# A two-block transformer kernel: two weight loads ahead of the key moves, attention values copied bank by bank, mLSTM transposes and convolution low parts moved

## The reference

```python
def hybrid_mixer(hc, hx, w_in, gate_b, mnorm_g, conv_w, w_out, with_ctx):   # first block, layer 0
    q, k, v, o, g, gb, gc, u = jnp.split(h @ w_in, splits, axis=-1)
    ...   # forward and backward mLSTM in chunks, from q, k, v and the gates g
    hn = rms_norm(h.transpose(0, 2, 1, 3), mnorm_g.reshape(ML_HEADS, ML_DV))
    m_out = (hn * sigmoid(o)).reshape(bsz, n, ML_HEADS * ML_DV)
    c_out = gb * short_conv(gc * u, conv_w)
    return jnp.concatenate([m_out, c_out], axis=-1) @ w_out

def attention_mixer(hc, hx, w_in, q_g, k_g, w_out, cos, sin, with_ctx):     # first block, layer 1
    ...   # rms_norm of 16 query and 4 key heads of 64, rope, softmax over 768 keys, @ w_out

def second_block(x, mem, ...):
    ...   # stick-breaking attention, a 31-tap convolution and an SSM side by side, then
    ...   # cross attention to 256 memory tokens, then a gated MLP
```

## Time and profile before

| | us |
|---|---|
| runs shown, median of 3 (lowest to highest) | 2702.88 (2699.74 to 2705.7) |
| the profiled execution, its own time | 2689.14 |
| its span | 2687.4 |
| TensorE busy in it | 2438.8 (91%) |
| VectorE, GpSimd, ScalarE busy | 1492.7, 1128.6, 968.7 |
| mean granted clock of TensorE | 0.953 of full |

### The profile page before, as it was taken

The page is one execution under the profiler, slowest core; times in us unless marked ns, Lnnn a source line. Parts: engine busy times, 40 slices in busy tenths (PEclk is TensorE's granted clock), DMA queues, the critical chain, the costliest instruction groups (busy, mean ns, idle before and its releaser), DMA issues.

```text
span 2687.4 us, 31912 instructions
## 1 busy us (share of the span) xinstructions
PE 2438.8 (91%) x11638; PEld 1970.9 (73%) x11638; DVE 1492.7 (56%) x1997; ACT 968.7 (36%) x1513; POOL 1128.6 (42%) x853
## 2 busy tenths in 40 slices
PE   7999877999999997599989999897888888899999
PEld 6888766888888886466768888676644665688887
DVE  7756756746464634888552122469488444452433
ACT  5212233413131326567452233443444353432322
POOL 1423112535343422277634467355453231344444
PEclk7999988999999998899999999999999899999999
DMA  6333102333333321411222232132200120232323
GB/s 229 128 108 118 40 31 95 118 110 109 109 109 109 109 94 40 108 36 43 75 77 94 95 97 92 60 111 94 94 0 1 55 69 26 73 100 93 101 90 107
DMA packets 68822, 231.69 MB, mean 86 GB/s; under 512 B 8048, under 2 KB 10992, under 8 KB 68592
## 3 DMA queue, kind: packets, MB, share of 16 engines
q1 hardware_dynamic: 68720, 230.35, 26.4%
HBM read 219.57 MB, written 2.10 MB: 82 GB/s over the span
## 4 chain that ended last, share of the span: by engine, by line
PE 48%; issue 25%; POOL 13%; DVE 10%; ACT 3%; SPq 1%; DMA 1%; POOLq 0%; DVEq 0%; ACTq 0%
PE PS L671 33%; POOL HL L530 12%; PE PS L689 5%; DVE RD L2341 2%; PE PS L1115 1%; PE PS L708 1%; DVE ADJ L1964 1%; PE PS L939 1%; DVE SM L2325 1%; PE PS L1208 1%; PE PS L1104 1%; SPq L484 0%; PE PS L1080 0%; PE PS L1123 0%; DMA EARLY<-adastream 0%
## 5 line engine op out<-in xcount | busy, mean ns | idle before, releaser
L530 POOL TENSOR_TENSOR HL<-RAW,HL 128x512 fp32r<-128x512 f32 x614 | 900.8, 1489 | 1374.0 <-ACT HL L1253 1373.6
L671 PE MATMUL PS<-HA,HL 128*128 128x512 f32 (+1 forms) x2592 | 556.4, 367 | 18.1 <-DVE V L2115 5.0
L671 PE MATMUL PS<-HID,HL 128*128 128x512 f32 (+1 forms) x2832 | 561.8, 360 | 0.0
L671 PE MATMUL PS<-HB,HL 128*128 128x512 f32 (+1 forms) x2592 | 540.7, 361 | 0.0
L671 PEld LDWEIGHTS PS<-HID,HL 128*128 128x128 f32 x2832 | 478.3, 188 | 82.0
L671 PEld LDWEIGHTS PS<-HA,HL 128*128 128x128 f32 x2592 | 445.1, 190 | 109.7 <-issue 29.7
L1253 ACT ACTIVATE HL<-RAW 128x1024 fp32r<-128x1024 f32 x307 | 323.2, 1053 | 494.5 <-PE PS L671 381.7
L671 PEld LDWEIGHTS PS<-HB,HL 128*128 128x128 f32 x2592 | 442.5, 189 | 75.7
L1964 DVE CUSTOM_DVE_ANT_0 ADJ<-ADA,CB 128x1024 f32<-128x1024 f32 x160 | 265.7, 1661 | 8.0 <-DVE X L1886 2.7
L1886 DVE SCALAR_TENSOR_TENSOR X<-PS,MOD,X 128x256 f32<-128x256 f32 (+1 forms) x120 | 75.8, 659 | 329.5 <-PE PS L671 311.8
L689 PE MATMUL PS<-HA,HL 128*128 128x256 f32 (+1 forms) x576 | 137.6, 402 | 55.8 <-DVE HA L1867 43.6
(11 more groups left out here) (376 smaller groups left out, 2720.2 us busy)
## 6 DMA issues: line engine op xcount, KB each, us to landing
RAW<-wstream SPq DMA_DIRECT2D x307, 512.0 KB, 3.5
ADA<-adastream SPq DMA_DIRECT2D x80, 512.0 KB, 3.7
EARLY<-adastream SPq DMA_DIRECT2D x16, 512.0 KB, 14.3
QB<-QH SPq DMA_DIRECT2D x32, 128.0 KB, 2.3
X<-x_in SPq DMA_DIRECT2D x8, 384.0 KB, 6.2
QC<-QL SPq DMA_DIRECT2D x16, 128.0 KB, 2.3
out<-X SPq DMA_DIRECT2D x8, 256.0 KB, 2.3
X<-mem SPq DMA_DIRECT2D x1, 1024.0 KB, 6.3
```

Of the source, the lines that this page charges most:

```text
L530: a = pool.tensor_tensor(HL[:, t % RING, 1, half], RAW[:, t % RAW_RING, half], HL[:, t % RING, 0, half].bitcast(F32), ALU.subtract)
L671: mm = pe.matmul(bank(t % 2, r), w[:, wp, k * P:(k + 1) * P], a[:, ap, lo:hi], start=(k == 0 and (wp, ap) == (0, 0)), stop=(k == nk - 1 an ...
```

## The change

1. Values of layer 0. `gemm_wide` is replaced by `gemm_banks`: in the first of its tiles the banks that the tile before may still occupy (0 and 1) come last, and only there TensorE waits for that tile to be read; in all tiles the bank is the outer loop and the chunk the inner one; in the last tile each finished bank is signalled (`bank_done`). ScalarE copies each bank to V1 as it comes; VectorE's copies go.
2. mLSTM. `turn` comes behind `sums` in a slot; the last two `turn`s move into the output projection, ahead of chunks 7 and 0, two of the six go to bank 6; ScalarE makes the convolution's first high parts ahead of the last sum of squares; the four low parts of the convolution go from VectorE to GpSimd, ahead of its next weight tiles.
3. Key moves. The loads of tiles T_OUT1+2 and T_OUT1+3 are issued ahead of the moves.
4. Second block. Its values use `gemm_banks`, and VectorE copies bank by bank.

```diff
 CONV_ORDER = [2, 3, 0, 1]
+TURN_BANK = [7, 7, 7, 6, 7, 6]
...
-    stretch(t, T_OUT1 + 2)
+    stretch(t, T_OUT1 + RING)
...
             move(H(s // 2)[0:64, s % 2, 0:256], KH[p, c, 256 * i:256 * i + 256], "k_in")
-    stretch(T_OUT1 + 2, T_OUT1 + RING + 1)
+    weights(T_OUT1 + RING)
...
                                ALU.mult).then_inc(S("k_weighted"), 1)
+    for j, i in enumerate(CONV_ORDER):
+        pool.wait_ge(S("conv_hi"), j + 1)
+        pool.tensor_tensor(HB[:, i, 1, :], CO[:, i, :], HB[:, i, 0, :].bitcast(F32),
+                           ALU.subtract).then_inc(S("conv_lo"), 1)
...
                 for b, bk in zip(blocks, banks):
-                    for wp, ap in ((0, 0), (0, 1), (1, 0)):
-                        mm = pe.matmul(PS[:, bk, 0:width], H(k)[:, ap, b * P:(b + 1) * P],
-                                       HL[:, t % RING, wp, kk * width:(kk + 1) * width],
-                                       start=(k == 0 and (wp, ap) == (0, 0)),
-                                       stop=(k == KC - 1 and (wp, ap) == (1, 0)))
+                    mm = wide_product(t, k, kk, width, b, bk)
+            mm.then_inc(S("tile_done"), 1)
+    def wide_product(t, k, kk, width, b, bk):
+        for wp, ap in ((0, 0), (0, 1), (1, 0)):
+            mm = pe.matmul(PS[:, bk, 0:width], H(k)[:, ap, b * P:(b + 1) * P],
+                           HL[:, t % RING, wp, kk * width:(kk + 1) * width],
+                           start=(k == 0 and (wp, ap) == (0, 0)), stop=(k == KC - 1 and (wp, ap) == (1, 0)))
+        return mm
+    def gemm_banks(t0, n, blocks, banks):
+        width, per = 512, TILE // 512
+        narrow = PLAN[t0 - 1][1] != "W"
+        held = [bk for bk in banks if bk < 4 and bk // 2 == (t0 - 1) % 2] if narrow else []
+        pairs = list(zip(blocks, banks))
+        banks_free(t0, 0, wide=not narrow)
+        for j in range(n):
+            t = t0 + j
+            pe.wait_ge(S("w_lo"), t + 1)
+            if j == 0:
+                for b, bk in sorted(pairs, key=lambda x: x[1] in held):
+                    if bk in held:
+                        banks_free(t0, 0, wide=True)
+                    for kk in range(per):
+                        mm = wide_product(t, kk, kk, width, b, bk)
+            else:
+                for i, (b, bk) in enumerate(pairs):
+                    for kk in range(per):
+                        mm = wide_product(t, j * per + kk, kk, width, b, bk)
+                    if j == n - 1 and i < len(pairs) - 1:
+                        mm.then_inc(S("bank_done"), 1)
...
             pe.wait_ge(S("h_norm"), i + 1)
-            if i:
-                pe.wait_ge(S("h_out"), i)
+            if TURN_BANK[i] in TURN_BANK[:i]:
+                pe.wait_ge(S("h_out"), i - TURN_BANK[:i][::-1].index(TURN_BANK[i]))
             for h in range(ML_HEADS):
-                mm = pe.transpose(PS[:, 7, h * P:(h + 1) * P], HS[:, b, h, :], const(C_ID))
+                mm = pe.transpose(PS[:, TURN_BANK[i], h * P:(h + 1) * P], HS[:, b, h, :], const(C_ID))
...
         pe.wait_ge(S("free_A"), freed_by["A"][25])
-        for s in range(N_ML + 3):
+        for s in range(N_ML + 1):
...
                 decay_and_scores(s)
+            if 1 <= s:
+                sums(s - 1)
...
                 turn(DONE.index(s - 3))
-            if 1 <= s <= N_ML:
-                sums(s - 1)
+        return turn
...
     t += 5
-    gemm_wide(t, 4, 512, range(6), (0, 1, 2, 3, 5, 6))
+    gemm_banks(t, 4, (2, 3, 0, 1, 4, 5), (2, 3, 0, 1, 5, 6))
...
             row_turns()
-    mlstm()
+    turn = mlstm()
...
     def mix0_ready(k):
+        if k == 4 + CONV_ORDER[1]:
+            turn(4)
+        if k == 0:
+            turn(5)
...
         if i == 8:
-            gemm_wide(t, 4, 512, range(2, 6), (0, 1, 2, 3))
+            gemm_banks(t, 4, range(2, 6), (0, 1, 2, 3))
...
         elif i < 19:
-            gemm_wide(t, 4, 512, range(2), (0, 1) if i == 17 else (2, 3))
+            gemm_banks(t, 4, range(2), (0, 1) if i == 17 else (2, 3))
...
     for i in range(4):
-        tile(t)
+        if i < 3:
+            tile(t)
+        else:
+            high(t + AHEAD)
...
             act.activation(A8[0:36, :], RA[:, :], ACT.Copy).then_inc(S("row_hi"), 1)
+        if i == 3:
+            act.wait_ge(S("dve_once"), ONCE["v_ones"])
+            for j, (b, bk) in enumerate(((2, 2), (3, 3), (0, 0), (1, 1), (4, 5), (5, 6))):
+                if j < 5:
+                    act.wait_ge(S("bank_done"), j + 1)
+                else:
+                    act.wait_ge(S("tile_done"), t)
+                a = act.activation(V1[:, b, :, 0:ML_DV], by_head(PS[:, bk, :]), ACT.Copy)
+            a.then_inc(S("free_V"), 4)
...
             first_half(s - 1)
-        if s - 1 in DONE:
-            squares(DONE.index(s - 1))
...
                 high_conv(i)
+        if s - 1 in DONE:
+            squares(DONE.index(s - 1))
...
+    def bank_ready(base, i, n, tiles):
+        if i < n - 1:
+            dve.wait_ge(S("bank_done"), base + i + 1)
+        else:
+            dve.wait_ge(S("tile_done"), tiles)
...
                       ALU.subtract).then_inc(S("gate_rows"), 1)
-    dve.wait_ge(S("tile_done"), 9)
-    for i, bk in enumerate((0, 1, 2, 3, 5, 6)):
-        a = dve.tensor_copy(V1[:, i, :, 0:ML_DV], by_head(PS[:, bk, :]))
-    a.then_inc(S("free_V"), 4)
...
         dve.wait_ge(S("h_turn"), i + 1)
-        dve.tensor_tensor(HS[:, b, :, :], by_head(PS[:, 7, :]), OG[:, :, tok(b)], ALU.mult).then_inc(S("h_out"), 1)
+        dve.tensor_tensor(HS[:, b, :, :], by_head(PS[:, TURN_BANK[i], :]), OG[:, :, tok(b)], ALU.mult).then_inc(S("h_out"), 1)
...
-    def low_conv(j):
-        i = CONV_ORDER[j]
-        dve.wait_ge(S("conv_hi"), j + 1)
-        dve.tensor_tensor(HB[:, i, 1, :], CO[:, i, :], HB[:, i, 0, :].bitcast(F32),
-                          ALU.subtract).then_inc(S("conv_lo"), 1)
...
             state(s - 1)
-        if s == N_ML:
-            low_conv(0)
...
             normed(DONE.index(s - 2))
-        if s == N_ML + 1:
-            low_conv(1)
...
             low_h(DONE.index(s - 3))
-    for j in (2, 3):
-        low_conv(j)
...
         if i == 8:
-            dve.wait_ge(S("tile_done"), t + 12)
             for b in range(4):
+                bank_ready(5, b, 4, t + 12)
...
             g = i - 17
-            dve.wait_ge(S("tile_done"), t + 20 + 4 * (g + 1))
             for b in range(2):
+                bank_ready(8 + g, b, 2, t + 20 + 4 * (g + 1))
```

More of the change, by code:

```diff
@@ L70 @@
            ("ffng", 8), ("qs8", 1), ("lamr", 8), ("lami", 8), ("ldt", 8), ("ssd", 2)])
-ONCE = {n: i + 1 for i, n in enumerate(("eps_set", "prm_ready", "c_silu", "first_gains", "v_split"))}
+ONCE = {n: i + 1 for i, n in enumerate(("eps_set", "prm_ready", "c_silu", "first_gains", "v_ones", "v_split"))}
 ACT_ONCE = {n: i + 1 for i, n in enumerate(("rho_rows", "k_tok", "cols_read", "row_exp", "mask_set", "sel_set", "v_high", "att_fixed"))}
@@ L2048, in _ @@
             norm("0a", "cx", root=False)
-            dve.memset(V1[:, :, :, ML_DV:ML_DV + 1], 1.0)
+            dve.memset(V1[:, :, :, ML_DV:ML_DV + 1], 1.0).then_inc(S("dve_once"), 1)
             marks = const(C_ID).rearrange("p (q n) -> p q n", q=4)
```

## The result

| | before | changed |
|---|---|---|
| median of the runs timed together, us | 2701.31 (four runs, 2694.71 to 2705.7) | **2668.22** (four runs, 2664.12 to 2669.27) |
| profiled execution, us | 2689.14 | 2669.27 |
| its span, us | 2687.4 | 2667.5 |
| mean granted clock of TensorE | 0.953 | 0.956 |

The ratio is 0.9872 with a 95% interval of [0.9853, 0.989]: 33.1 us less by the medians, where 31.7 were forecast. On another chip, in five runs against eleven, it was 0.9874 [0.9851, 0.9898]. The two profiled executions are only 19.9 us apart, so the terms have to be read stage by stage; where the other 13 us lie is the subject of the last experiment.

What follows compares the result with a forecast made beforehand. TensorE and its weight-tile stream bound the kernel, so removed idle counts in full. Gains 9.2 + 3.4 + 5.4 + 4.5 + 8.6 + 0.6 = 31.7 us take the median 2702.9 to 2671; forecast range 2665 to 2678.

Steps and rivals of the forecast that it cites:

- 1, value tiles: First block's value tiles: TensorE's waits before and behind them shrink and tile 9's clock stays up; gain 9.2 us.
- 2, steps 5 and 6: mLSTM: sums no longer wait behind transposes, removing VectorE's 2.50 and 0.94 us idle; gain 3.4 us.
- 2, steps 11 and 12: mLSTM end: step 10's sums do not wait, so the last sums start earlier, ahead of the transpose; gain 5.4 us.
- 2, last sums to chunk 0: mLSTM into its output projection: chunk 0 starts 14.0 us after the last sums instead of 18.5; gain 4.5 us.
- 3, key moves: Before attention: ScalarE's 10.07 us wait for a weight load and VectorE's 8.70 go; gain 8.6 us.
- 4, second block: Second block: its value copies gain 0, the cross-attention values save one copy; gain 0.6 us.
- Term 2: mLSTM: sums ahead of transposes, with VectorE's queue becoming the limit; parts of 3.4, 5.4 and 4.5 us.
- rival (a): Ports: GpSimd's first two low parts block VectorE's last normalisations, 4.4 us together; gain 20 to 27; chance 0.12.
- Rival (b): Clock: mixer chunks 0 to 5 run at low clock, 25.4 us instead of 12.7; gain 19; chance 0.09.
- rival (c): Slower: the clock falls over the whole mLSTM stage; result 13 us slower, 2716; chance 0.02.
- what is late next: Before attention: moved keys land about 1124, but ScalarE's five us of constants fit before VectorE's need near 1131.

Runs made afterwards that it cites:

- the last experiment: Nothing changed: changed kernel profiled again (2669.69 us) and the kernel before three times more (2698.46, 2698.56 and 2703.96 us), compared stretch by stretch.
- the experiment: Changed kernel with the convolution's four low parts back on VectorE: 2662.33 us, ratio to before 0.9876.
- the one load ahead: Changed kernel with one weight tile's load ahead of the key moves instead of two: 2670.0 us, beside 2669.69.
- the reordered queue: Variant with low parts on VectorE, its queue behind the last sums interleaved and both last transposes ahead of chunk 7: 2664.26 us, ratio to before 0.9856.

## Why the prediction was right, and where it was not

Of the forecast 31.7 us the traces show, by stages, first profile against first profile:

| term | forecast | measured |
|---|---|---|
| 1, value tiles | 9.2 (6.5 to 9.5) | 9.40 |
| 2, steps 5 and 6 | 3.4 (0 to 6.4) | 4.5 |
| 2, steps 11 and 12 | 5.4 (3.7 to 7) | 5.6 |
| 2, last sums to chunk 0 | 4.5 (3 to 6) | 5.8, less 1.9 behind chunk 0 |
| 3, key moves | 8.6 (6 to 9) | 7.5 |
| 4, second block | 0.6 | 0.5 |
| sum | 31.7 | 31.4 |

The sum over the places of the change came out as forecast. 19.9 is what is left of it after a start that was 2.8 us later, an MLP 6.9 slower and some 2 in small pieces elsewhere; against the forecast's 2657.4 for the profiled execution the changed kernel's took 2669.27.

**Term 1** was right by each of its parts, with one fact short: the 2.44 us of idle ahead of the value tiles usually costs 1.6 to 1.7 more in clock, which the first profile of before did not show. The windows of the changed kernel give a clock of 1.00 for tile 9, where the earlier trace rows has 0.59:

```profile
135.30:142.00 6.70, 6.66 (x38) 5.92 (x39) 3.77 (x5) 0.85 (x1) 4.03 (x2) 1.00 0.33 109
...
343.70:356.40 12.70, 7.32 (x37) 5.98 (x34) 10.24 (x22) 5.24 (x15) 3.60 (x2) 0.87 0.00 0
356.40:371.30 14.90, 14.52 (x72) 12.28 (x72) 1.23 (x3) 2.58 (x4) 6.13 (x4) 0.89 0.12 36
```

**Term 2** was right in its mechanism. Steps 5 and 6 were taken at 12 us and came to 10.07, 5.5 less than before; steps 7 to 10 took 19.24 for 18.23 and gave 1.0 of that back, which leaves the 4.5 of the table. VectorE's idle time, from which the 3.4 was taken, was thus not the whole of the loss. The tail was right by its number and wrong in one step: chunk 6 started 2.9 behind the last sums, as forecast, and took 3.9, but what followed was not a chain of two chunks, two transposes and three operations. VectorE's queue from the last sums to chunk 0 was the longer, busy 10.24 of 12.70 us. And rival (a) was partly there, inside a term that still came out better than forecast: the ports did stretch VectorE, by 2.5 us of the 4.4 at most, and the experiment shows that the low parts could have stayed where they were. Rival (b), the low clock over chunks 0 to 5, came for about 1.8 us of its 12.7 (chunks 0 to 3 in 10.28 instead of 8.48), rival (c) not at all: steps 5 to 10 ran at 1.00, steps 11 and 12 at 0.84 where they had run at 0.68, and the stretch from the last sums to chunk 0 at 0.87 where it had been 0.63 (360.13 to 378.65 before).

**Term 3** was somewhat too large, 8.6 for 7.5 and inside its range, at the step "what is late next". It named the moved keys and let ScalarE's constants fit before VectorE needs them; the one load ahead shows that the keys cost nothing and that VectorE's own 22.33 us of work is the bound, reached with 1.1 us less to gain.

**Term 4** held: the copies of the second block's values start straight behind the taps as in the earlier trace rows, and TensorE waits 4.61 us for them, as it did before (at 1850.80):

```profile
1828.66 2.48 DVE L2484 COPY VS<-PS 128x512 f32<-128x512 f32 x4
...
1831.29 2.61 PE L676 MATMUL PS<-HA,HL 128*128 128x256 f32 x12 [4.61 <-DVE VS L2484]
```

The cross-attention values gave half a microsecond in the wait behind them, before and now:

```profile
1926.26 3.41 PE L1036 MATMUL PS<-CY,SMALL 128*128 128x512 f32 x4 [2.07 <-DVE CH L2482]
```

```profile
1908.03 1.95 PE L1073 MATMUL PS<-CY,SMALL 128*128 128x512 f32 x4 [1.54 <-DVE CH L2522]
```

The stretch between the two norm sums shows 0.3 of it (434.49 to 434.17). No run tried this edit alone.

The forecast of the median, 2671, rested on carrying the 13.7 us between the profile of before and its median over unchanged. That was luck as much as judgement: the changed kernel's profile lies at its own median, so the difference did not carry over, and the forecast for the profile was 12 us too low. The four profiles of before explain the gain of the medians in part. Against their means (266.78, 71.81, 18.05 and 35.88 by the table's rows, and 1.65 lost behind chunk 0) the change gains 9.7, 9.9, 5.3 and 7.4, less 1.7: 30.8. The second block adds 3.2, since its long stretches (442.15 and 438.71) did not come in either profile of the changed kernel, and the MLP takes 4.4. That makes 29.6 of the 33.1 between the medians; where the other 3.5 lie is open, with two to four profiles of either kernel. Whether the change makes the slow case of the second block rarer stays open: a variant of the changed kernel, the one with the transposes ahead, had 442.18 there.

## What to carry to other kernels

Where one engine issues in order, put the work whose input is ready ahead of the work that waits, and take care that a buffer is handed over bank by bank as its last use ends; an idle stretch of TensorE can be worth more than its length, 2.44 and 1.7 of low clock behind it here, while one of 0.84 cost only itself. Before moving work to a spare engine, ask whether the engine it leaves is the bound there and whether the two will hold each other up: here the reordered queue gave 2.9 us where the move gave 0.2. And compare stretches of the timeline, on more than one execution of either kernel, before an edit is given or denied its microseconds.

## What the runs showed that was not expected

The MLP's matmuls of 128x512 take 391 ns or 399 at the same granted clock of 1.00, for a whole row of tiles at a time; in 24 matmuls of alternating sizes that is 4.16 or 4.24 us. Which of the two comes changed between executions of one kernel on one chip (556.81, 563.45 and 565.69 for the stretch), while four kernels on one chip all had the fast rate in the MLP and four on another all the slow one. One of the first four had the slow rate in the tiles ahead of the second norm and the fast one in the MLP of the same execution. Nothing in the traces names the cause.

A VectorE operation on 128x4 elements, 0.15 us alone, took up to 1.75 us beside GpSimd's 128x768 subtraction, so its size gives it no shelter: it ended when GpSimd's instruction ended.

An idle stretch of 2.44 us ahead of the value tiles was enough in five of six profiles that have it for the next two tiles to take 18.2 us instead of 16.5, with a granted clock of 0.80 to 0.83 over their first 8 to 10 us, and one of 0.84 us ahead of tile 9 in none of eight for tile 9 to run low.
